# Routing gates of the dense half placed in memory by indirect adding transfers instead of one-hot products

## The reference, cut to what matters

```
def peer_block(hb, w_q, keys, u, v):
    T, K = hb.shape[0], PEER_TOPK                      # K = 16, PEER_HEADS = 8, PEER_KEYS = 128
    q = (hb @ w_q).reshape(T, PEER_HEADS, 2, PEER_DQ // 2)
    s = jnp.einsum('thpd,pkd->thpk', q, keys)
    top_s, top_i = lax.top_k(s, K)                     # 16 of 128 on either side
    cand_s = top_s[:, :, 0, :, None] + top_s[:, :, 1, None, :]    # reshaped to K * K
    cand_i = top_i[:, :, 0, :, None] * PEER_KEYS + top_i[:, :, 1, None, :]
    best_s, pos = lax.top_k(cand_s, K)                 # 16 of 256
    idx = jnp.take_along_axis(cand_i, pos, axis=-1)    # expert number, 0 .. 16383
    g = jax.nn.softmax(best_s, axis=-1)
    act = jax.nn.gelu(jnp.einsum('thkd,td->thk', u[idx], hb))
    return jnp.einsum('thk,thkd->td', g * act, v[idx])
```

## Time and profile before

| | |
|---|---|
| median of 3 runs | 3494.57 us |
| lowest, highest | 3482.6, 3504.53 us |
| span of the profiled execution | 3492.1 us |
| PE busy | 3192.0 us, 91% |
| DVE busy | 2453.1 us, 70% |
| ACT busy | 1676.2 us, 48% |
| POOL busy | 1545.0 us, 44% |

### The profile page before, as it was taken

How to read it: one execution, slowest core, us unless ns; L and a number is a source line. 1 busy time by engine, 2 the same in 40 slices (tenths; PEclk the granted TensorE clock), 3 DMA queues, 4 the chain that set the end, 5 groups by cost and what they waited for, 6 DMA issues and landing times.

```text
span 3492.1 us, 49503 instructions
## 1 busy us (share of the span) xinstructions
PE 3192.0 (91%) x14956; PEld 2577.3 (74%) x14956; DVE 2453.1 (70%) x5180; ACT 1676.2 (48%) x2260; POOL 1545.0 (44%) x1329
## 2 busy tenths in 40 slices
PE   6999889979999999999989988898998899889986
PEld 3799556768888878888867777676777677777765
DVE  4631555536888886666638888788887787878878
ACT  2210244323333244444436666666666666666655
POOL 2000335134333233333346666566666666666653
PEclk8999789989999999999999999999999999999998
DMA  5610000223323234544567878787777778778877
GB/s 203 211 52 24 16 25 1 79 86 106 111 88 110 81 116 160 208 163 168 199 228 253 273 257 279 246 273 258 265 262 264 249 264 268 257 263 267 270 246 243
DMA packets 325789, 645.32 MB, mean 185 GB/s; under 512 B 169264, under 2 KB 170688, under 8 KB 322752
## 3 DMA queue, kind: packets, MB, share of 16 engines
q1 hardware_dynamic: 233280, 337.63, 29.0%
q0 software_dynamic: 91264, 272.96, 23.2%
q10 hardware_dynamic: 1152, 33.55, 2.3%
HBM read 568.52 MB, written 75.50 MB: 184 GB/s over the span
## 4 chain that ended last, share of the span: by engine, by line
PE 26%; DVE 14%; issue 12%; another core or an unknown queue 5%; ACT 4%; DVEq 1%; ACTq 0%; DMA 0%; SPq 0%
PE ga_dots L1470 8%; DVE total L2266 6%; PE ex_y L2142 5%; PE ex_dots L2132 4%; PE ga_dots L1474 4%; PE gm_prod L1929 3%; DVE total L2235 3%; ACT ex_vhi L2202 2%; PE ex_dots L2135 2%; DVE px_ulo L1520 2%; DVE ex_wlo L2223 1%; DVE ex_vlo L2223 1%; ACT ex_prod L2183 1%; DVE ex_dots L2246 1%
## 5 line engine op out<-in xcount | busy, mean ns | idle before, releaser
L2183 ACT ACTIVATE ex_prod<-ex_ring,ex_present 128x512 f32<-128x512 f32 x1024 | 693.3, 686 | 542.3 <-DVE total L2266 366.9
L2102 POOL DMA_INDIRECT ex_ring<-peer_v_dram,sp_row x512 | 537.6, 1050 | 472.2 <-ACT ex_prod L2183 345.2
L2266 DVE TENSOR_TENSOR total<-total,ex_prod 128x512 f32<-128x512 f32 x1016 | 671.3, 682 | 22.2 <-ACT ex_prod L2183 11.6
L2097 POOL DMA_INDIRECT ex_pick<-act_scratch,sp_place x512 | 492.7, 962 | 177.0 <-issue 156.2
L1460 POOL TENSOR_TENSOR px_ulo<-px_u,px_uhi 128x1024 fp32r<-128x1024 f32 x128 | 310.2, 2426 | 549.6 <-ACT px_uhi L1454 549.4
L2142 PE MATMUL ex_y<-ex_vhi,ex_whi 128*128 128x512 f32 x768 | 321.2, 418 | 150.0 <-DVE total L2235 134.4
L2132 PE MATMUL ex_dots<-h_hi_b,px_uhi 128*128 128x512 f32 x1024 | 421.2, 411 | 4.2 <-PEq L1887 4.1
L2132 PE MATMUL ex_dots<-h_lo_b,px_uhi 128*128 128x512 f32 x1024 | 417.1, 407 | 0.0
L2235 DVE TENSOR_TENSOR total<-total,ex_y 128x512 f32<-128x512 f32 x378 | 258.2, 683 | 210.6 <-remote 163.9
L1987 DVE TENSOR_SCALAR gm_b_hot<-gm_iota,second_T,gate_T 128x128 f32<-128x128 f32 x512 | 258.5, 575 | 169.3 <-PE gm_prod L1929 166.5
L2142 PE MATMUL ex_y<-ex_vhi,ex_wlo 128*128 128x512 f32 x768 | 313.6, 408 | 6.8 <-issue 6.7
(11 more groups left out here) (299 smaller groups left out, 6450.4 us busy)
## 6 DMA issues: line engine op xcount, KB each, us to landing
px_u<-peer_u_dram SPq DMA_DIRECT2D x256, 512.0 KB, 3.6
px_v<-peer_v_dram SPq DMA_DIRECT2D x128, 512.0 KB
gate_scratch<-gm_out ACTq DMA_DIRECT2D x8, 4096.0 KB, 11.9
ex_g<-gate_scratch SPq DMA_DIRECT2D x128, 256.0 KB
act_scratch<-ga_act SPq DMA_DIRECT2D x72, 256.0 KB, 2.1
w_in_raw<-w_ada_dram SPq DMA_DIRECT2D x64, 256.0 KB, 4.1
act_scratch<-ra_act SPq DMA_DIRECT2D x56, 256.0 KB, 2.2
w_ada_half<-w_ada_dram SPq DMA_DIRECT2D x4, 2048.0 KB, 14.0
```

Of the source, the lines that this page charges most:

```text
L2097: nc.gpsimd.indirect_dma_start(weights[:, i:i + 1], None, places, bass.IndirectOffsetOnAxis(ap=picks[:, i:i + 1], axis=0)).then_inc(pick_i ...
L2102: nc.gpsimd.indirect_dma_start(ring[:, i], None, rows, bass.IndirectOffsetOnAxis(ap=which[:, RING * s + i:RING * s + i + 1], axis=0)).then ...
L2183: nc.scalar.activation(prod[:, h], ring[:, i, h * HALF:(h + 1) * HALF], ACT.Copy, scale=present[:, b, i:i + 1]).then_inc(prod_ready, 1)
L2266: nc.vector.tensor_tensor(total[:, t, at], total[:, t, at], prod[:, h], ALU.add).then_inc(row_added, 1)
```

## The change

`gate_matrix` is gone, with its one-hot tiles, products, copies, and transposes, and so is the barrier before it. `route` now holds all 128 chunks of the sparse half: 12 in each head, and 32 behind the heads (`TAIL`).

`gate_scratch` has a new layout, [128, 128, 512] (second key, first key, token). Class `Clear` writes it full of zeros during the mixer, 16 stores of 2 MB by SP: eight in `gated_linear`, behind its two loads, and eight in `stick_breaking`, behind the load of the output weights, with a wait for all.

In `route` DVE makes, behind the gates of a head, the addresses of the dense half's picks (`dense_expert`, `dense_place`). GpSimd then issues for each head 64 indirect transfers (16 picks x 4 tiles), each of which **adds** 128 gates, one per partition, to 128 single elements of `gate_scratch`: 512 in all. Before those of a head it waits until those of the head before have landed.

The low parts of the chunks (`split_low`) move from POOL to DVE, as two instructions of 512 columns each with the form of L1520. They stand at written-out places in DVE's program: four in each `top16`, that is 12 in a head, none in the key part, except in the first and last head. DVE is four chunks ahead (`LEAD`): head h makes those of chunks 12h + 4 to 12h + 15. The gates of head h - 1 move to the start of head h, ahead of the wait for the scores, and ACT's exponents move in front of `scores(0)`. `experts` loads `ex_g` as rows of 2 KB.

```diff
-def stick_breaking(nc, k, d, fm, tm, o, w_out):
+def stick_breaking(nc, k, d, fm, tm, o, w_out, clear):
...
                 w_out.load(sp, 0, w_out.first[0])
+                clear.part(sp, 1)
+                clear.done(sp)
...
                 for dst, name in ((near, "gla_near"), (gains, "qk_gain_rep")):
                     sp.dma_start(dst[:], d[name]).then_inc(gl_in, 16)
+                clear.part(sp, 0)
...
+                clear.zero(pool)
...
+    def zero(self, pool):
+        self.nc.gpsimd.memset(self.zeros[:], 0.0).then_inc(self.zero_ready, 1)
+
+    def part(self, sp, which):
+        each = KEYS // (2 * self.PIECES)
+        sp.wait_ge(self.zero_ready, 1)
+        for piece in range(which * self.PIECES, (which + 1) * self.PIECES):
+            dst = self.scratch[piece * each:(piece + 1) * each].rearrange("a i t -> i a t")
+            sp.dma_start(dst, self.zeros[:].unsqueeze(1).to_broadcast([P, each, TBD])).then_inc(self.cleared, 16)
+
+    def done(self, sp):
+        sp.wait_ge(self.cleared, 16 * 2 * self.PIECES)
...
-PER_HEAD = 6
-PER_STEP = 18
-STEPS = 4
-AFTER_HEADS = 8
-ROUTED = PH * PER_HEAD + AFTER_HEADS
+PER_HEAD = 12
+LEAD = 4
...
-    def split_low(self, eng, n, c, first):
-        eng.wait_ge(self.uhi_ready, n + 1)
+    def split_low(self, dve, n, c, first):
+        dve.wait_ge(self.uhi_ready, n + 1)
         if not first:
-            eng.wait_ge(self.dots_ready, n - 1)
-        eng.tensor_tensor(self.ulo[:, c], self.u[:, c], self.uhi[:, c].bitcast(F32),
-                          ALU.subtract).then_inc(self.ulo_ready, 1)
+            dve.wait_ge(self.dots_ready, n - 1)
+        for kk in (slice(0, KD // 2), slice(KD // 2, KD)):
+            last = self.nc.vector.scalar_tensor_tensor(self.ulo[:, c, kk], self.uhi[:, c, kk].bitcast(F32), -1.0,
+                                                       self.u[:, c, kk], ALU.mult, ALU.add)
+        last.then_inc(self.ulo_ready, 1)
...
+                def place_gates(h):
+                    pool.wait_ge(dense_ready, h + 1)
+                    for t in range(NB_TILES):
+                        if h:
+                            pool.wait_ge(gate_placed[t], 16 * TOPK * h)
+                    for q in range(TOPK * h, TOPK * h + TOPK):
+                        for t in range(NB_TILES):
+                            i = q * NB_TILES + t
+                            nc.gpsimd.indirect_dma_start(
+                                elements, bass.IndirectOffsetOnAxis(ap=places[:, i:i + 1], axis=0),
+                                gate[:, NA + t, q:q + 1], None, compute_op=ALU.add).then_inc(gate_placed[t], 16)
...
-                head(0, False)
-                with pool.Fori(1, PH - 1) as h:
-                    head(h, False)
-                head(PH - 1, True)
+                for h in range(PH):
+                    if h + 1 < PH:
+                        for p in range(2):
+                            split(h + 1, p)
+                    if h:
+                        place_gates(h - 1)
+                place_gates(PH - 1)
+                for t in range(NB_TILES):
+                    pool.wait_ge(gate_placed[t], 16 * P)
...
                         if p:
+                            if not first:
+                                exponents(h - 1)
                             scores(0)
...
+                    nc.vector.scalar_tensor_tensor(dense_expert[:], second_key[:, NA:, at], float(KEYS),
+                                                   first_key[:, NA:, at], ALU.mult, ALU.add).then_inc(vec, 1)
+                    dve.wait_ge(vec, count + 4)
+                    for t in range(NB_TILES):
+                        last = nc.vector.tensor_scalar(dense_place[:, at, t], dense_expert[:, t], float(TBD),
+                                                       sparse.token[:, t:t + 1], ALU.mult, ALU.add)
+                    last.then_inc(dense_ready, 1)
...
+                    def low_half(count=1):
+                        for _ in range(count):
+                            n = low[0]
+                            ahead.split_low(dve, PER_HEAD * h + n, n % 2, False)
+                            low[0] += 1
...
                                 last = nc.vector.max(values[:, t, part], src[:, t])
+                            low_half()
                             link(last)
...
+                            low_half()
                             link(last)
...
+                    if not first:
+                        gates(h - 1, base)
+                        done[0] += 4
                     dve.wait_ge(score_ready, 2 * h + 2)
...
+                        if first or final:
+                            low_half(1 if first else 2)
...
-                    sp.dma_start(g[:, c].rearrange("p (b t) -> p b t", b=NB), src).then_inc(g_in[c], 16)
+                    src = scratch[n] if isinstance(n, int) else scratch[bass.ds(n, 1)].rearrange("a i t -> (a i) t")
+                    sp.dma_start(g[:, c], src).then_inc(g_in[c], 16)
...
-    gates = nc.dram_tensor("gate_scratch", [NB, P, KEYS, TB], F32)
+    gates = nc.dram_tensor("gate_scratch", [KEYS, P, TBD], F32)
```

More of the change, by code:

```diff
@@ L1606, in _ @@
                 chunks(PH - 1)
-                for n in range(PH * PER_HEAD, ROUTED):
-                    ahead.load_and_store(sp, n, n % 2, n < ROUTED - 2)
-                ahead.stores_done(sp, ROUTED)
+                for n in TAIL:
+                    more = n + 2 < KEYS
+                    if not more:
+                        sp.wait_ge(ahead.ulo_ready, n + 1)
+                        stream.load_u(sp, n % 2, n % 2)
+                    ahead.load_and_store(sp, n, n % 2, more)
+                for c in range(2):
+                    stream.load_v(sp, c, c)
             @block.gpsimd
             def _(pool):
+                elements = scratch[:].rearrange("a i t -> (a i t)").unsqueeze(1)
+                places = dense_place[:].rearrange("p q t -> p (q t)")
                 def split(h, p):
@@ L1743, in _, with gates @@
                 head(PH - 1, False, True)
-                for n in range(PH * PER_HEAD, ROUTED):
-                    if n == ROUTED - 3:
-                        exponents(PH - 1)
[L1747 to L1750, removed]
-                    src = (q_ps[:], s_ps[:].rearrange("p t c -> p (t c)"), q_ps[:])[n]
-                    act.wait_ge(turned_ready, n + 1)
-                    nc.scalar.activation(dst[:], src[:, 0:TBD], ACT.Copy).then_inc(copied, 1)
+                for n in TAIL:
+                    ahead.gelu(act, n, n % 2, n // 2, False)
+                    if n + 2 < KEYS:
+                        ahead.split_high(act, n + 2, n % 2, n // 2 + 1, False)
+                    if n == PH * PER_HEAD + LEAD + 2:
+                        exponents(PH - 1)
+                act.wait_ge(ahead.dots_ready, KEYS - 1)
+                stream.high_u(act, 0, 0)
             @block.vector
             def _(dve):
-                def gates(h, count, signal=None):
+                def gates(h, count):
                     dve.wait_ge(exp_ready, h + 1)
@@ L1798, in head @@
                     nc.vector.tensor_copy(top_key[:], top_at[:]).then_inc(score_used, 1)
-                    if not first:
-                        gates(h - 1, base + done[0])
-                        done[0] += 3
-                        dve.wait_ge(vec, base + done[0])
                     for part, a, z, wide in ((cand[:, :, 0:WIDE], 0, ROWS, TOPK), (cand[:, :, WIDE:], ROWS, TOPK, SHORT)):
@@ L1831, in head @@
                         link(nc.vector.tensor_reduce(dst[:, :, bass.ds(h * TOPK, TOPK)], pick[:], AX.X, ALU.add))
-                    assert done[0] == LINKS - (3 if first else 0), done
+                    assert done[0] == LINKS - (4 if first else 0), done
+                    assert low[0] == PER_HEAD + LEAD + (4 if final else 0), low
+                for c in range(2):
+                    ahead.split_low(dve, c, c, True)
                 dve.wait_ge(const_in, 32)
+                dve.wait_ge(token_ready, 1)
                 head(0, True)
-                with dve.Fori(1, PH) as h:
+                with dve.Fori(1, PH - 1) as h:
                     head(h, False)
-                gates(PH - 1, PH * LINKS - 3, picked)
+                head(PH - 1, False, True)
+                opened = PH * PER_HEAD + LEAD + 4
+                ahead.split_low(dve, opened, opened % 2, False)
+                gates(PH - 1, PH * LINKS - 4)
+                for n in range(opened + 1, KEYS - 2):
+                    ahead.split_low(dve, n, n % 2, False)
                 nc.vector.scalar_tensor_tensor(expert[:], second_key[:, 0:NA], float(KEYS), first_key[:, 0:NA],
@@ L1997, in _ @@
+                for n in range(KEYS - 2, KEYS):
+                    ahead.split_low(dve, n, n % 2, False)
+                dve.wait_ge(ahead.dots_ready, KEYS - 1)
                 stream.low_u(dve, 0, 0)
@@ L2387, in trunk @@
                 o = sbm("mix_out", [P, NT, D])
[L2388 removed]
```

(3 more changed lines are left out.)

186 lines of the change are left out of this document (28 added, 158 removed).

## The result

The changed kernel takes 3628.19 us in the median of 4 runs (3612.2 to 3632.12), the kernel before on the same chip 3490.9 (4 runs). The ratio is 1.0377, 95% interval [1.0348, 1.0405]: slower by 137 us where I had forecast 120 faster, and outside the range. The profiled execution took 3630.04 us, 1.7 above its span.

What follows compares the result with a forecast made beforehand. PE's queue was taken to bound `route` and `gate_matrix`. -126.9 + 9 + 0 + 2 - 4 - 5 = -125 against the 3492.1 us span gave 3367, plus 2.5 for the runs' median: 3370 us; range 3325 to 3490 (0.79), its own 3345 to 3395.

Steps and rivals of the forecast that it cites:

- Removed products and seam, -126.9: Joining `route` and `gate_matrix` drops one-hot products (117.1 us) and the seam (9.8 us) from PE's queue: -126.9 us.
- DVE's new order, +9: In `route`, PE loses about 1.0 to 1.5 us in each of 7 heads to late low parts: +9, bounds +5 and +65.
- DVE becomes late: Rival: in `route`, descriptor making delays DVE's key part by 4 to 10 us a head, seven times: about 3425 us; chance 0.13.
- GpSimd, 0: 512 adding transfers in the joined stage cost 1.27 to 1.45 us each, hidden under PE's work: 0 us.
- POOL end = 917 + 512p: When POOL ends in the joined stage if it never waits, p being the price of one adding transfer.
- the price is for making descriptors: Argument against GpSimd as bound: element reads are as quick as those of 4 KB rows, so descriptor making sets the price.
- both thresholds, 1.47 and 1.70: Transfer price in us: hidden behind PE up to 1.47; at 1.70 all gain is gone. Chances: 0.06 between, 0.21 beyond.
- GpSimd becomes the bound: Rival: adding makes transfers dearer, so POOL ends the joined stage; 3597 us at p = 1.9; chance 0.06 between thresholds, 0.21 beyond.
- 50 us of slack: A weight split behind the earlier head's transfers in POOL's queue has some 50 us to spare at 1.27 to 1.45.
- Beside DVE, 2 us a head: In the router, DVE's short port-holding forms, some ten a head, slow descriptor writing by 2 us a head; sum unchanged.
- Clearing, +2: Zero stores queued ahead of `sw_bias` on SP's queue may delay `sliding_window`: +2 us, bounds 0 and +35.
- `experts`, -9: `experts` gains -4 from an earlier first gate load and -5 from `ex_g` as 2 KB rows.

Runs made afterwards that it cites:

- three tiles, first build: Changed kernel with three dense tiles by adding transfers, the fourth by one-hot products in a separate short step: 3443.27 us, ratio 0.9863 to the kernel before.
- the last build: Three tiles by adding transfers, the fourth by one-hot products, with one stream of chunks over both steps: 3423.47 us, ratio 0.9795 to the kernel before.

## Why the prediction was wrong

- **Removed products and seam, -126.9: held.** With no transfers the stage ends at 1665.0; my sum for it was 1790.1 - 126.9 + 9 = 1672.
- **DVE's new order, +9: too high, under its lower bound of 5.** PE waited for low parts 7 times, 4.6 us in all without transfers and 2.9 with them; I had said two waits a head and 7 to 10 us. The rival "DVE becomes late" is out.
- **GpSimd, 0: this step failed.** It said: "I take 1.27 to 1.45, by the nearest row, where it costs 0". The first gates were ready at 888.2, as I had counted, and the rule POOL end = 917 + 512p holds: with p = (849.8 + 154.3) / 512 = 1.96 it gives 1921, and the stage ended at 1922.4. With 64 elements (p = 1.84) it gives 1859, measured 1858.3; with the spaced plain writes (p = 1.80) 1840, measured 1837.8. That it fits so closely is partly luck: I had put twelve splits behind the first transfer, 29 us, where ten stand, 26.3 us in all, and left out 4.5 us of waits for landing. What failed was p. The nearest row was a read with no add. Taking the add away brought the median from 1.556 back to 0.962 us. So the argument "the price is for making descriptors" was right in that POOL's own time is the price and not the landing, and hid that an adding transfer is dearer to make. My bounds were 1.27 and 2.5; the value taken lay at the low end, and both thresholds, 1.47 and 1.70, lay inside them. Between ends so far apart on either side of a sign, the chance of 0.21 beyond 1.70 was too low.
- **The rival named for this, "GpSimd becomes the bound", is what happened**, at 3597 for p = 1.9 against 3628 for 1.96: 0.06 x 512 = 31 us is the difference. What I had said would show it did: POOL back to back, PE at the barrier. I had expected the splits to have 50 us of slack. At 64 x 1.96 + 6 = 131 us a head they had none, and part of the loss appears there.
- **Beside DVE, 2 us a head: nearer 7.** The mean of a transfer is 1.660, the median 1.556: 512 x 0.104 = 53 us for the ones that took longer, up to 3.6 us. The trace tells which these are. 209 of the 512 run beside an instruction of DVE with two inputs from SBUF (`tensor_tensor`, `scalar_tensor_tensor`), and they hold all of the 53 us over the median; the other 303 come to the median in the mean. Some 27 us fall beside the low parts that this change gives to DVE, 24 beside the two products of `ro_pick`, as here (POOL, then DVE):

```profile
966.00 1.56 POOL L1663 DMA_INDIRECT gate_scratch<-pick_gate,ro_dense_place  x1 [0.30 <-issue]
967.86 3.62 POOL L1663 DMA_INDIRECT gate_scratch<-pick_gate,ro_dense_place  x1 [0.30 <-issue]
...
967.76 2.29 DVE L1877 TENSOR_TENSOR ro_pick<-ro_half,ro_iota 128x2048 f32<-128x2048 f32 x1
970.16 2.29 DVE L1880 TENSOR_TENSOR ro_pick<-ro_pick,ro_top_key 128x2048 f32<-128x2048 f32 x1
```

The Trainium skill (SBUF — State Buffer, "Who interferes with whom") says that a VectorE instruction with two SBUF inputs contends with a GpSimd instruction that reads SBUF. The trace agrees, if making a transfer reads its addresses, which lie in SBUF (`dense_place`). It is not the form that I had looked for (casts, copies and `tensor_scalar`). That they stand together is measured; no run takes the DVE instructions away. These 53 us alone would not have turned the sign: p = 1.86 also lies beyond 1.70.
- **Clearing, +2: it cost nothing.** 16 stores of 2 MB landed in a median of 18.8 us, `sw_bias` was issued at 415.7 and landed in 3.1, and the instruction behind it ran at 422.4 (before at 423.3). PE's first router product started at 753.8, before at 755.0.
- **`experts`, -9: nothing measured.** Before it took 1702.0 us. The variants took 1696 (three tiles, first build) to 1711 (plain writes for two tiles), the changed kernel 1705.9, the last build 1704.3, with no order in them. Packets under 512 bytes fell from 169264 to 112032 (73728 of these are the adding transfers' own; without them 38304 are left) and the DMA share from 0.79 to 0.76, as I had said, and the time did not follow. No gain from the 2 KB rows shows, which fits the wait for `ex_g` of 2.3 us in all.

## What to carry to other kernels

Work that is moved to an idle engine is priced by count times the period of one operation, and the period has to be that of the very kind: a read of the same shape was 35% too cheap for an adding write. If the threshold at which a new bound appears lies between your own bounds, measure that one number first; a stage rule such as 917 + 512p then gives the result at once. When a whole replacement fails by a known count, move only the part that fits under the cover: three tiles of four gave 2% where four cost 4%.

## What the runs showed of the hardware

- An indirect transfer of 128 single elements that adds takes POOL 1.56 us to make and 0.30 to the next; one that only writes 0.96 and 0.30. With 64 elements the adding one takes 1.42: by a line through the two sizes about 1.28 us are fixed and 2.1 ns go with each element. Beside a DVE instruction with two inputs from SBUF it takes longer, up to 3.62 us.
- Plain single-element writes made every 1.26 us hold up everything beside them for tens of us (PE busy 34 of 85 us from 880 to 965, at a granted clock of 0.69), while the DMA engines are recorded as nearly idle and the writes' own packets keep pace; made every 1.67 us or more they do not. The adding ones, every 1.96 us, were never seen to do it; they can't be made faster here, so whether they would is open. What holds the others up was not found. The counts of packets differ: 32 on queue q0 for a plain one, (107648 - 91264) / 512, and 144 for an adding one, (164992 - 91264) / 512.
